# Hybrid encoder layer: the meta tokens' high and low parts in one stationary matrix, and the recurrent stage's transpositions and state updates one step on in TensorE's program

## The reference

```python
hn = rms_norm(h, g_mix_pre[l])              # 1040 rows of 1024
proj = hn @ w_in[l]                         # among others hq, hf_fwd, hf_bwd, hi, hg
...
# per head and direction, chunk by chunk; b is the running sum of log f in the chunk
S = exp(b_last) * S + einsum('bhcd,bhcv->bhdv', k_c * exp(b_last - b), v_c)
o = (inside the chunk) + einsum('bhtd,bhdv->bhtv', q_c * exp(b), S)
```

## Time and profile before

| | us |
|---|---|
| median of 3 runs | 2178.48 |
| lowest, highest | 2176.82, 2178.69 |
| time of the profiled execution | 2178.05 |
| its span | 2176.3 |
| PE busy | 2125.7 (98%), 11536 matmul records |
| DVE busy | 1283.7 (59%) |
| ACT busy | 948.1 (44%) |
| POOL busy | 398.4 (18%) |

### The profile page before, as it was taken

One profiled execution on the slowest core, in us unless ns is written; L12 is line 12 of the kernel. 1 busy time (PEld: TensorE's weight loads), 2 busy tenths in 40 slices (PEclk: granted clock), 3 DMA queues, 4 the chain that ended last, 5 costly groups with the idle time before them and its releaser, 6 DMA issues. The chain is left out here.

```text
span 2176.3 us, 30857 instructions
## 1 busy us (share of the span) xinstructions
PE 2125.7 (98%) x11536; PEld 1796.0 (83%) x11536; DVE 1283.7 (59%) x1966; ACT 948.1 (44%) x1550; POOL 398.4 (18%) x242
## 2 busy tenths in 40 slices
PE   8999999999999999989999999999999999999999
PEld 8988888888888888778888888777788888888886
DVE  3403664756647557447777777568866766651431
ACT  6324354443554525455555555545432323243422
POOL 1110000000000000021111111020055454524443
PEclk9999999999999999999999999999999999999999
DMA  5112111120120111130111111254322222354452
GB/s 187 60 54 68 35 64 51 47 68 34 63 68 34 63 56 41 49 137 1 49 48 51 47 50 42 102 192 148 129 83 78 97 79 73 122 183 164 148 184 96
DMA packets 79101, 181.82 MB, mean 84 GB/s; under 512 B 6976, under 2 KB 27776, under 8 KB 77344
## 3 DMA queue, kind: packets, MB, share of 16 engines
q1 hardware_dynamic: 79008, 180.56, 23.8%
HBM read 142.13 MB, written 38.40 MB: 83 GB/s over the span
## 5 line engine op out<-in xcount | busy, mean ns | idle before, releaser
L88 PE MATMUL h_bank<-hn_hi,w_hi 128*128 128x512 f32 (+2 forms) x952 | 371.0, 390 | 2.8 <-ACT raw L716 1.6
L90 PE MATMUL h_bank<-hn_hi,w_lo 128*128 128x512 f32 (+2 forms) x952 | 353.4, 371 | 0.0
L89 PE MATMUL h_bank<-hn_lo,w_hi 128*128 128x512 f32 (+2 forms) x952 | 353.0, 371 | 0.0
L88 PEld LDWEIGHTS h_bank<-hn_hi,w_hi 128*128 128x128 f32 x952 | 179.0, 188 | 33.2 <-issue 8.7
L90 PEld LDWEIGHTS h_bank<-hn_hi,w_lo 128*128 128x128 f32 x952 | 178.7, 188 | 27.7
L89 PEld LDWEIGHTS h_bank<-hn_lo,w_hi 128*128 128x128 f32 x952 | 179.2, 188 | 26.5 <-issue 3.8
L716 ACT COPY raw<-h_bank 128x512 f32<-128x512 f32 (+2 forms) x119 | 63.8, 543 | 279.8 <-PE h_bank L90 249.4
L2148 ACT CAST w_hi<-w_raw 128x1024 fp32r<-128x1024 f32 x79 | 82.7, 1049 | 203.7 <-PE f_bank L90 192.9
L895 DVE TENSOR_TENSOR w_lo<-w_raw,w_hi 128x1024 fp32r<-128x1024 f32 x52 | 63.5, 1221 | 138.2 <-ACT w_hi L696 138.2
L1132 POOL MEMSET ckv_hi<- 128x224 f32 x1 | 0.3, 284 | 778.8 <-POOLq L585 778.8
L1453 ACT CAST prob_hi<-a_bank 128x512 fp32r<-128x512 f32 x144 | 83.1, 588 | 131.5 <-PE a_bank L1721 131.1
(11 more groups left out here) (411 smaller groups left out, 5374.1 us busy)
## 6 DMA issues: line engine op xcount, KB each, us to landing
w_raw<-in_w_ffn SPq DMA_DIRECT2D x82, 512.0 KB, 3.5
w_raw<-in_w_hgrn SPq DMA_DIRECT2D x54, 512.0 KB, 3.2
raw_up<-in_w_ffn SPq DMA_DIRECT2D x18, 512.0 KB, 4.6
hidden<-gate_blocks SPq DMA_DIRECT2D x34, 256.0 KB, 2.0
w_raw<-in_w_out SPq DMA_DIRECT2D x15, 512.0 KB, 3.3
w_raw<-in_w_head SPq DMA_DIRECT2D x9, 512.0 KB, 5.7
X<-in_x SPq DMA_DIRECT2D x8, 520.0 KB, 9.0
values<-values_h SPq DMA_DIRECT2D x32, 128.0 KB, 1.7
```

The costliest lines, as they stand in the source:

```text
L88: pe.matmul(out, wh, xh, start=start, stop=False)
L89: pe.matmul(out, wh, xl, start=False, stop=False)
L90: return pe.matmul(out, wl, xh, start=False, stop=stop)
```

## The change

**Values.** `meta_hi` and `meta_lo` become one matrix `meta`: the 16 high columns, the 16 low columns, then zeros. A step of a meta unit is now two matmuls (`meta` by `w_hi`, `meta` by `w_lo`) in place of three. Rows 0 to 15 of the bank hold the high tokens' products, rows 16 to 31 the low tokens', and nothing adds them: all 32 rows are scaled, evicted, stored and loaded again. For the scaling, DVE copies the 16 sums of squares once more behind the others, and `token_sums` waits for that copy and takes 32 columns in its last matmul.

**Recurrent stage.** The 32 rows are added up by the matmul of updates 0, whose contraction is 32 rows long now. For that the meta keys must stand twice: DVE subtracts them twice, ACT's exponential is 1056 wide in place of 1040, DVE multiplies them twice, and turn 0 transposes 32 columns.

**Order.** Turns 0 to 4 and updates 0, 1 and 2 come one step later in `PE_STEPS`. Inside 0 and all behind it keep their steps.

```diff
-        meta_hi, meta_lo = sb("meta_hi", [P, KT, P], F32R), sb("meta_lo", [P, KT, P], F32R)
+        meta = sb("meta_parts", [P, KT, P], F32R)
...
-                    rows = P if tile < TT else META
+                    rows = P if tile < TT else 2 * META
...
-                    act.copy(meta_hi[:, :, 0:META], hn_hi[:, :, SEQ:L].bitcast(F32)).then_inc(padded, 1)
-                    act.copy(meta_lo[:, :, 0:META], hn_lo[:, :, SEQ:L].bitcast(F32)).then_inc(padded, 1)
+                    act.copy(meta[:, :, 0:META], hn_hi[:, :, SEQ:L].bitcast(F32)).then_inc(padded, 1)
+                    act.copy(meta[:, :, META:2 * META], hn_lo[:, :, SEQ:L].bitcast(F32)).then_inc(padded, 1)
...
                 add(KT - 1)
+                dve.wait_ge(added, KT - 1)
+                dve.tensor_copy(t.raw[:, 5 * L:5 * L + META], square_sum[:, SEQ:L]).then_inc(added, 1)
...
-                pool.memset(meta_hi[:, :, META:].bitcast(F32), 0.0).then_inc(padded, 1)
-                pool.memset(meta_lo[:, :, META:].bitcast(F32), 0.0).then_inc(padded, 1)
+                pool.memset(meta[:, :, 2 * META:].bitcast(F32), 0.0).then_inc(padded, 1)
...
-                    left = {x: of[:, k, tokens(tile)] if tile < TT else meta[:, k, :]
-                            for x, of, meta in (("hi", hn_hi, meta_hi), ("lo", hn_lo, meta_lo))}
-                    return three(pe, place(n), left["hi"], left["lo"], vw_hi[part % 2][:, k, :],
-                                 vw_lo[part % 2][:, k, :], k == 0, k == KT - 1)
+                    right_hi, right_lo = vw_hi[part % 2][:, k, :], vw_lo[part % 2][:, k, :]
+                    if tile == TT:
+                        pe.matmul(place(n), meta[:, k, :], right_hi, start=(k == 0), stop=False)
+                        return pe.matmul(place(n), meta[:, k, :], right_lo, start=False, stop=(k == KT - 1))
+                    return three(pe, place(n), hn_hi[:, k, tokens(tile)], hn_lo[:, k, tokens(tile)], right_hi,
+                                 right_lo, k == 0, k == KT - 1)
...
-                    pe.wait_ge(added, KT - 1)
+                    pe.wait_ge(added, KT)
...
-PE_STEPS = [(36, "turn", 0), (38, "turn", 1), (39, "updates", 0), (40, "turn", 2), (42, "updates", 1),
-            (43, "turn", 3), (45, "turn", 4), (47, "updates", 2), (51, "inside", 0), (53, "updates", 3),
+PE_STEPS = [(37, "turn", 0), (39, "turn", 1), (40, "updates", 0), (41, "turn", 2), (43, "updates", 1),
+            (44, "turn", 3), (46, "turn", 4), (48, "updates", 2), (51, "inside", 0), (53, "updates", 3),
...
+        ends_twice, meta_again = factor[FWD][:, 0:L + META], factor[FWD][:, L:L + META]
...
-                    act.activation(ends[dd], ends[dd], ACT.Exp).then_inc(ends_exp.sem, 1)
+                    whole = ends_twice if dd == FWD else ends[dd]
+                    act.activation(whole, whole, ACT.Exp).then_inc(ends_exp.sem, 1)
...
-                        dve.tensor_tensor(ends[dd][:, SEQ:L], cum[dd][:, L - 1:L].to_broadcast([P, META]),
-                                          cum[dd][:, SEQ:L], ALU.subtract)
+                        for at in (ends[dd][:, SEQ:L], meta_again):
+                            dve.tensor_tensor(at, cum[dd][:, L - 1:L].to_broadcast([P, META]), cum[dd][:, SEQ:L],
+                                              ALU.subtract)
...
+                    if dd == FWD:
+                        dve.tensor_tensor(meta_again, meta_again, key[dd][:, SEQ:L], ALU.mult)
                     dve.tensor_tensor(ends[dd], ends[dd], key[dd][:], ALU.mult).then_inc(ends_done.sem, 1)
...
-                        pe.matmul(u_bank[:, 0:P], ends_meta_t[:], values[0:META, TT, :], start=True,
+                        pe.matmul(u_bank[:, 0:P], ends_meta_t[:], values[0:2 * META, TT, :], start=True,
                                   stop=True).then_inc(u_done.sem, 1)
```

More of the change, by code:

```diff
@@ L388, in step @@
                     part, tile = units[n]
-                    left = {x: of[:, k, tokens(tile)] if tile < TT else meta[:, k, :]
-                            for x, of, meta in (("hi", hn_hi, meta_hi), ("lo", hn_lo, meta_lo))}
-                    return three(pe, place(n), left["hi"], left["lo"], vw_hi[part % 2][:, k, :],
-                                 vw_lo[part % 2][:, k, :], k == 0, k == KT - 1)
+                    right_hi, right_lo = vw_hi[part % 2][:, k, :], vw_lo[part % 2][:, k, :]
[4 more added lines that the diff above has]
+                                 right_lo, k == 0, k == KT - 1)
                 def token_sums():
                     pe.wait_ge(consts_in, 16)
-                    pe.wait_ge(added, KT - 1)
+                    pe.wait_ge(added, KT)
                     for tile in range(UNITS):
-                        rows = P if tile < TT else META
-                        last = pe.matmul(sum_bank[0:rows, 2 * tile:2 * tile + 2], square_sum[:, tokens(tile)],
+                        rows = P if tile < TT else 2 * META
+                        of = square_sum[:, tokens(tile)]
+                        if tile == TT:
+                            of = t.raw[:, 4 * L + SEQ:5 * L + META]
+                        last = pe.matmul(sum_bank[0:rows, 2 * tile:2 * tile + 2], of,
                                          t.const("ones")[:, 0:2], start=True, stop=True)
@@ L422, in _ @@
                         token_sums()
-                        pe.wait_ge(padded, 4)
+                        pe.wait_ge(padded, 3)
                     if tile == 0:
@@ L608, in both @@
                             sp.dma_start(values[:, 0:TT, :], t.d_v[:, 0:TT, bass.ts(hi, P)]).then_inc(v_in.sem, 16)
-                            sp.dma_start(values[0:META, TT, :],
-                                         t.d_v[0:META, TT, bass.ts(hi, P)]).then_inc(v_in.sem, 16)
+                            sp.dma_start(values[0:2 * META, TT, :],
+                                         t.d_v[0:2 * META, TT, bass.ts(hi, P)]).then_inc(v_in.sem, 16)
                             sig_done.wait(sp, h, 6)
@@ L661, in ends_copy @@
                     if i == 0:
-                        act.copy(ends_meta_t[:], ends_bank[0:META, 0:P]).then_inc(ends_copied.sem, 1)
+                        act.copy(ends_meta_t[:], ends_bank[0:2 * META, 0:P]).then_inc(ends_copied.sem, 1)
                         return
@@ L918, in turn @@
                         ends_copied.wait(pe, h, 5, lag=1)
-                        pe.matmul(ends_bank[0:META, 0:P], ends[FWD][:, SEQ:L], t.const("ident"), start=True,
+                        pe.matmul(ends_bank[0:2 * META, 0:P], factor[FWD][:, SEQ:L + META], t.const("ident"), start=True,
                                   stop=True).then_inc(ends_turned.sem, 1)
```

6 lines of the change are left out of this document (3 added, 3 removed).

## The result

| | before | the change |
|---|---|---|
| median, us | 2177.74 (20 runs, 2175.24 to 2179.2) | 2182.31 (20 runs, 2179.69 to 2186.9) |
| profiled execution, us | 2178.05 | 2183.65 |
| its span, us | 2176.3 | 2181.6 |

The ratio is 1.0023, with a 95% interval of 1.0017 to 1.0029: the change makes the kernel 4.6 us slower. The forecast was +1.4 us and 2179.9, with a range up to 2183.0. The range holds the result, but by luck: its upper end was set by a rival (*Turn 1's wait stays*) that the traces rule out, and the time was lost to something else. The page says how much less PE has to do than in the earlier trace rows: 32 matmuls and 32 weight loads fewer, 2 us less busy time, and 5.3 us more span. The third part of the page, on the DMA queues, has a row for packets of instructions, which no term of the prediction counts; before, it said 61.

A forecast was written before the change was run, and what follows sets the result against it. PE, busy 2125.7 of 2176.3 us, was taken to bound the kernel, with waits for DVE at the change. Values -1.9 and order +3.3 gave +1.4 us, a median of 2179.9 us, range 2176.3 to 2183.0.

The forecast's parts named there:

- Turn 1's wait stays: Rival, recurrent stage: ACT's copy comes later by more than the step; +3.5 us, 2182.0 us; chance 0.09.
- Point 1: Values stage: 32 matmuls fewer, half the saving swallowed by waits of the row sum and unit 21; -1.9 us.
- The DMA comes in time: Rival, values stage: ACT's 3.45 us DMA wait was chance, tiles start 1.5 us earlier; -0.1, 2178.4 us; chance 0.15.
- point 2: Values stage: DVE's extra copy of the sums is covered by PE's first eight units, 1.2 us to spare; cost 0.
- point 3: Recurrent stage: doubled meta keys' added work is covered by turn 1's later step; 0, or 0.2 us per head uncovered.
- Point 4: Recurrent stage, the order: later turn 4 delays inside 0, tied 5.87 us behind: 5.4 - 2.1 = +3.3 us.
- (a): Recurrent stage: turn 1, a step later, no longer waits for ACT's copy of the meta keys; -2.1 us.
- What is late next is all behind inside 0, which shifts with it: Recurrent stage: later PE and DVE pieces keep their distances, no other wait absorbs the shift; 8 x 0.68 = 5.4 us.
- The move is free: Rival, recurrent stage: inside 0 isn't tied to turn 4, only gains stay; -4.0 us, 2174.5 us; chance 0.08.
- The clock falls: Rival: PE's idling ahead of inside 0 lowers its clock, 1.7 us per head; +14.8 us, 2193.3 us; chance 0.04.

The follow-up runs named there:

- e6: Kernel before with 192 PE instructions added by splitting 96 matmuls in the first round of projections: 2185.20 us, +7.4 us, ratio 1.0035.
- e3: The change with inside 0 also moved one step later, to step 52: 2179.27 us, +1.7 us against the kernel before, ratio 1.0013.
- e7: The change with inside 0 at step 52 and 64 instructions given back by narrow matmul splits: 2178.95 us, +1.2 us against before, ratio 1.0008.
- e2: Kernel before with only the change's moved steps (the order): 2180.41 us, +2.9 us, ratio 1.0014.
- e8: Kernel before with the change's order and inside 0 at step 52, without the values' edit: 2178.56 us, +0.8 us, ratio 1.0004.
- e12: Kernel before with 256 PE instructions added, one whole block, by splitting 128 matmuls of 512 columns: 2179.46 us, +1.7 us, ratio 1.001.
- e1: The change without its moved steps, so the values' edit with the old order: 2182.52 us, +5.0 us against the kernel before, ratio 1.0023.
- e4: The changed kernel unaltered, measured again: 2182.89 us, +5.4 us against the kernel before, ratio 1.0023.
- e5: The change with 64 instructions given back by splitting 32 matmuls of 384 and 272 columns: 2181.37 us, +3.6 us against before, ratio 1.0019.
- e9: The change with 64 instructions given back by splitting 32 matmuls of 512 columns: 2179.74 us, +2.0 us against before, ratio 1.0011.
- e10: The change with inside 0 at step 52 and 64 instructions given back by 512-column splits: 2176.76 us, -1.0 us against before, ratio 0.9996.
- e11: The values' edit with the old order, 64 instructions given back by 512-column splits: 2178.87 us, +1.2 us against before, ratio 1.0004.

## Why the prediction was right or wrong

**Point 1, the values.** The waits of the row sum and of unit 21 grew as said. The two sides of the gain can be seen in the recurrent stage's beginning, if like traces are compared. Where the clock was low near 37 to 38 us, the kernels without the values' edit begin it at 0 and -0.4 (before, e6), those with it at -2.5 and -2.3 (e3, e7): a gain of 2.2 us. Where it wasn't low there, those without the edit begin at -2.2, -1.3 and -1.8 (e2, e8, e12), those with it at -3.0 to -3.5 (the change, e1, e4, e5, e9, e10, e11): 1.5 us. The forecast of 1.9 lies between. The rest of the change's -3.5 is the rival *The DMA comes in time*, and no gain of the change. The prediction gave it 0.15, as a chance of the DMA's. The traces of the old values stage tie it to the clock instead: ACT's wait for the DMA is 3.45 and 3.58 us with the low stretch near 38 us (before, e6), and 1.8 to 2.1 without (e2, e8, e12).

**Points 2 and 3** held: neither cost anything. The copy of point 2 wasn't held up (0.17 us), so its cover of 1.2 us wasn't needed; an eviction of 32 rows took 456 ns on average and one of 128 rows 471, so the added rows are off the path as said. The missing cover of point 3 shows only in e1, with 0.25 us a head.

**Point 4, the order**, held in each number: 5.87 us in all heads, 7.4 us for the forecast 7.5, heads 0.3 to 0.5 us further apart, 3.26 us lost in the recurrence and 2.9 us in e2, for +3.3. But (a), turn 1's 2.1 us, isn't a gain that can be had by itself: in e8 the waits are gone and the heads are no shorter.

**The step that failed** stands behind both sums, as "What is late next is all behind inside 0, which shifts with it", and in point 1 as 32 matmuls whose only effect is their time. A missing term, not one mis-sized: 32 matmuls are also 64 instructions of PE's program, and the program is itself read by DMA. The diff moved each later packet to another place of the work, onto two bursts of weight loads that ACT and then PE wait for. In the traces that is 2.03 + 1.95 us for the change; by the medians, giving the 64 instructions back is worth 2.6 us from the change to e9, 2.7 from e3 to e10 and 3.8 from e1 to e11, each with 0.5 us for the splits against it. The forecast with this term, 1.4 + 2.6 + 0.5, makes +4.5 for the measured +4.6. That the sum agrees so well with the median is partly luck: the traces alone would give 4.0 for the term, and the early beginning of 1.5 us and the clock near 970 stand against each other in them.

The Trainium skill, "Runtime: NRT & Kernel Launch", section "Instruction fetch mechanics", tells of blocks of 16 KiB or 256 instructions, which the sequencer fetches over a DMA queue of its own, and calls the cost of a boundary mostly hidden. The size agrees with these runs (packets of 16 KB; 256 added instructions restore the places, 192 don't). The cost agrees only for PE's own supply: in all fourteen traces PE's sequencer is named as a releaser of PE only at three barriers between stages, with the same 1.4, 1.2 and 1.1 us in each. It isn't hidden where the packet meets a burst of loads with a waiting engine behind it.

**The rivals.** *The move is free* and *Turn 1's wait stays* are ruled out by 5.87 and 1.81 to 1.93 us. *The clock falls* didn't happen where it was priced: PE's waits of 0.9 us ahead of inside 0 left the clock at full in all eight heads. But a stretch near 970 shows in eight of the traces and not in the other six, and between 921.70 and 974.97 those eight lost 0.6 to 1.3 us, the others nothing; the change's 1.28 is among them. Whether the change makes it more likely, or its place in time does, these runs leave open. So does how a packet of 16 KB can hold up transfers of 512 KB by 1.8 us. The tail of the burst, at 15 to 30 GB/s with a height of over 400, would fit one of the 16 engines being behind the others, but the trace doesn't say which engine carried what, so this isn't shown.

One slip of the prediction's sums changes nothing: 2178.4 less 2 is 2176.4, not 2176.3.

## What to carry to other kernels

Count instructions as well as time: a removed or added matmul shifts every later packet of the engine's instructions against the work, and a loss of one to three microseconds can appear a thousand microseconds behind the edit. When an untouched stage gets slower, look in the DMA view of that window for an instruction packet, and test by adding harmless instructions up to a whole block. A piece that another one is tied to at a fixed distance is moved together with it or not at all, and even then the gain is only there if nothing behind it takes it back.

## What the runs showed of the hardware that was not expected

- One 16 KB packet of instructions among transfers of 512 KB made them land in 6.5 us in place of 4.7 (`lw_raw`) and in 6.2 in place of 4.6 (`w_raw<-in_w_out`).
- Splitting a matmul of 512 columns into two of 256 cost 0.016 us each (e12: 2.1 us for 128, from the recurrent stage's beginning to 216 us). Halves of 192 and 136 columns cost 0.06 us each (e5: 2.0 us for 32, the order's 0.5 taken off).
- A DVE subtraction of 16 columns took 4.60 us beside POOL's subtraction of 4.61, and 0.17 us in the kernel before, where it ended as POOL's began.
- Outside PE's two loops there is one packet of instructions for each 254 to 257 instructions of PE, its sequencer's included; while the loops run there is none for 469 and 235 us (before).
